# Two-block transformer layer pair on one core: where the token-form units of the second mixing accumulate

## What is computed

```python
u = rms_norm(h, ln_pre_mix[i])
proj = u @ w_in[i]
q_a, k_a, v_a, qkv_b, z_b, b_b, a_b, gate_a, gate_b = jnp.split(proj, IN_SPLITS, axis=-1)
qa = apply_rope(to_heads(q_a, 8), cos, sin)
ka = apply_rope(to_heads(k_a, 8), cos, sin)
y_a = from_heads(moba_attention(qa, ka, to_heads(v_a, 8)))        # plain causal attention at 256 tokens
qkv_b = jax.nn.silu(causal_depthwise_conv_2(qkv_b, conv_w[i]))    # 4 taps
q_b, k_b, v_b = jnp.split(qkv_b, 3, axis=-1)
o_b = gated_delta_rule(l2_norm(q_b), l2_norm(k_b), v_b, g_log, beta)
y_b = rms_norm(o_b, gdn_norm[i]) * jax.nn.silu(z_b)
merged = sigmoid(gate_a) * (y_a @ w_proj_a[i]) + sigmoid(gate_b) * (y_b @ w_proj_b[i])
```

## Time and profile before

| | us |
|---|---|
| median of the runs (3) | 1023.41 |
| the profiled execution | 1024.26 |
| its span, first to last instruction | 1022.0 |
| TensorE busy | 921.7 (90%) |
| VectorE busy | 584.3 (57%) |
| ScalarE busy | 523.7 (51%) |
| GpSimd busy | 133.2 (13%) |

### The profile page before, as it was taken

One profiled execution on the slowest core, in us unless ns is written; L12 is line 12 of the kernel. 1 busy time (PEld: TensorE's weight loads), 2 busy tenths in 40 slices (PEclk: granted clock), 3 DMA queues, 4 the chain that ended last, 5 costly groups with the idle time before them and its releaser, 6 DMA issues.

```text
span 1022.0 us, 16777 instructions
## 1 busy us (share of the span) xinstructions
PE 921.7 (90%) x6490; PEld 850.6 (83%) x6490; DVE 584.3 (57%) x865; ACT 523.7 (51%) x901; POOL 133.2 (13%) x122
## 2 busy tenths in 40 slices
PE   4996789999997988996898999998988999999977
PEld 4985589999996988996798988888976999999956
DVE  4576465555556556666546656463656555555555
ACT  5486454444447645554546363726336644444453
POOL 1000030000000000038536363300000000000000
PEclk9998989999998999999999999998999999999979
DMA  9631286656553444443212131312653555565611
GB/s 307 235 125 41 83 181 200 203 168 202 186 184 120 140 139 138 131 158 124 63 50 95 43 123 41 124 43 87 202 179 120 189 182 198 171 205 167 217 68 41
DMA packets 106940, 144.88 MB, mean 142 GB/s; under 512 B 2968, under 2 KB 94360, under 8 KB 106896
## 3 DMA queue, kind: packets, MB, share of 16 engines
q1 hardware_dynamic: 104608, 137.60, 42.0%
q0 software_dynamic: 1968, 6.02, 2.2%
q10 hardware_dynamic: 320, 0.66, 0.2%
HBM read 143.22 MB, written 1.05 MB: 141 GB/s over the span
## 4 chain that ended last, share of the span: by engine, by line
PE 75%; DVE 11%; ACT 9%; issue 3%; POOL 1%; DMA 1%; ACTq 0%; DVEq 0%; POOLq 0%
PE ps L1577 13%; PE ps L1579 13%; PE ps L1578 13%; PE ps L1583 8%; PE ps L1585 8%; PE ps L1584 8%; DVE wl L1090 3%; ACT wh L603 3%; PE ps L1897 2%; PE ps L1908 1%; PE ps L1912 1%; DVE R L1127 1%; PE ps L1729 1%; DVE h L1133 1%; DVE xTl L1117 1%
## 5 line engine op out<-in xcount | busy, mean ns | idle before, releaser
L1090 DVE TENSOR_TENSOR wl<-w_raw,wh 128x1024 fp32r<-128x1024 f32 x258 | 323.1, 1257 | 314.9 <-ACT wh L603 314.0
L1577 PE MATMUL ps<-xTh,wh 128*128 128x256 f32 (+1 forms) x1160 | 337.9, 291 | 13.3 <-ACT R L815 6.0
L1578 PE MATMUL ps<-xTl,wh 128*128 128x256 f32 (+1 forms) x1160 | 328.0, 283 | 0.0
L1579 PE MATMUL ps<-xTh,wl 128*128 128x256 f32 (+1 forms) x1160 | 327.8, 283 | 0.0
L603 ACT ACTIVATE wh<-w_raw 128x1024 fp32r<-128x1024 f32 x258 | 271.0, 1053 | 109.5 <-PE ps L1585 82.0
L1577 PEld LDWEIGHTS ps<-xTh,wh 128*128 128x128 f32 x1160 | 221.2, 191 | 18.9 <-ACT R L815 6.7
L1578 PEld LDWEIGHTS ps<-xTl,wh 128*128 128x128 f32 x1160 | 220.5, 190 | 2.1 <-issue 1.2
L1579 PEld LDWEIGHTS ps<-xTh,wl 128*128 128x128 f32 x1160 | 221.0, 191 | 0.0
L1583 PE MATMUL ps<-wh,y 128*128 128x512 f32 x224 | 89.4, 399 | 4.0 <-DVE y L1527 4.0
L1585 PE MATMUL ps<-wh,y 128*128 128x512 f32 x224 | 88.7, 396 | 0.0
L1584 PE MATMUL ps<-wl,y 128*128 128x512 f32 x224 | 88.3, 394 | 0.0
(11 more groups left out here) (337 smaller groups left out, 1331.7 us busy)
## 6 DMA issues: line engine op xcount, KB each, us to landing
w_raw<-in_w_in_dram SPq DMA_DIRECT2D x43, 1024.0 KB, 5.2
w_raw<-in_w_ff_dram SPq DMA_DIRECT2D x32, 1024.0 KB, 5.4
w_raw<-in_w_ffn_gate_dram SPq DMA_DIRECT2D x11, 1024.0 KB, 5.3
w_raw<-in_w_ffn_up_dram SPq DMA_DIRECT2D x11, 1024.0 KB, 5.3
w_raw<-in_w_ffn_down_dram SPq DMA_DIRECT2D x11, 1024.0 KB, 4.8
w_raw<-in_w_out_dram SPq DMA_DIRECT2D x8, 1024.0 KB, 4.9
w_raw<-in_w_proj_a_dram SPq DMA_DIRECT2D x4, 1024.0 KB, 4.9
w_raw<-in_w_proj_b_dram SPq DMA_DIRECT2D x4, 1024.0 KB, 5.0
```

Of the source, the lines that this page charges most:

```text
L1090: TT(split_view(wl, pu % UNITS, layout), raw_unit(SLOT[p], j, layout), split_view(wh, pu % UNITS, layout).bitcast(F32), ALU.subtract).then ...
L1577: mm(out, wh_, xh, start=first, stop=False)
L1578: mm(out, wh_, xl, start=False, stop=False)
L1579: return mm(out, wl_, xh, start=False, stop=last)
```

## The change

The token-form units no longer use the two unit banks. In the attention rounds (and in the set of units ahead of them) they accumulate in `acc[:, 0]` and `acc[:, 1]`, the banks of the scores; in the delta-rule rounds in `ma` and `mb`. So they neither wait for the unit banks nor fill them. A new semaphore `tok_out` counts ScalarE's copies of token-form results. TensorE waits for it where the borrowed banks are used next: the scores (stage 1 of an attention round), the sums of squares (stage 1 of a delta-rule round), `g_rows` and `out_transposes`. Before token-form units of a delta-rule round start, TensorE waits for `yb_lo` (or `o2_lo`) and `dt_out`, which say that `ma` and `mb` were read. The table of bank counts leaves the token form out. The number and size of all matmuls, copies and transfers is the same.

```diff
-            elif to in ("tok", "high") and j == 1:
+            elif to == "high" and j == 1:
...
+        tok_out = sem("token_rows_copied")
...
                 elif c == 7:
                     for t in range(NT):
-                        act.activation(va[:, t, :], fm[:, t, 0:S], ACT.Copy).then_inc(emptied[t], 1)
+                        ins = act.activation(va[:, t, :], acc[:, t, 0:S], ACT.Copy)
+                    ins.then_inc(tok_out, 1)
...
                     for t in range(NT):
-                        act.activation(zr[:, t, :], fm[:, t, 0:S], ACT.Copy).then_inc(emptied[t], 1)
+                        ins = act.activation(zr[:, t, :], acc[:, t, 0:S] if first else ps[:, 6 + t, 0:S], ACT.Copy)
+                    ins.then_inc(tok_out, 1)
...
                 if s == 15:
-                    act.wait_ge(emptied[0], along(EMPTIED0, 2 * P_GDN + 8, 8, a))
-                    act.wait_ge(emptied[1], along(EMPTIED1, 2 * P_GDN + 8, 8, a))
+                    act.wait_ge(tok_out, a + (PAIRS + 1))
...
-            def tok_steps(pu, off, stride=0, i=0):
+            def tok_steps(pu, off, banks, free, stride=0, i=0):
                 unit_ready(pu, stride, i)
                 j = pu % 2
                 if j == 0:
-                    bank_ready(0, pu, stride, i)
-                    bank_ready(1, pu, stride, i)
+                    free()
...
-                        last = three_tok(fm[:, t, 0:S], ...
+                        last = three_tok(banks[t], ...
...
+            def score_banks_free():
+                pass
+
+            def pair_steps(kinds, fu, stride, i, banks=(acc[:, 0, 0:S], acc[:, 1, 0:S]), free=score_banks_free):
...
             def moba_stage(s, a):
                 if s == 1:
                     pe.wait_ge(rope_out, a + 1)
+                    pe.wait_ge(tok_out, a + 1)
...
                         pe.wait_ge(sq_out, a * 2 + (n + 1))
+                        pe.wait_ge(tok_out, PAIRS + 1)
...
                 if s == 9 and not (isinstance(a, int) and a == PAIRS - 1):
+                    pe.wait_ge(tok_out, a + (PAIRS + 1))
                     g_rows(a + 1)
                 if s == 13 and not (isinstance(a, int) and a == 0):
+                    pe.wait_ge(tok_out, a + (PAIRS + 1))
                     out_transposes(a - 1)
...
+            def norm_banks_free(a):
+                def free():
+                    if isinstance(a, int) and a == 0:
+                        pe.wait_ge(o2_lo, PAIRS)
+                    else:
+                        pe.wait_ge(yb_lo, a)
+                    pe.wait_ge(dt_out, a + 2)
+                return free
+
             def pair_round(weave, stage, kinds, fu, a):
-                steps = pair_steps(kinds, fu, 8, a)
+                if weave is GDN_WEAVE:
+                    steps = pair_steps(kinds, fu, 8, a, (ma[:, 0:S], mb[:, 0:S]), norm_banks_free(a))
+                else:
+                    steps = pair_steps(kinds, fu, 8, a)
```

More of the change, by code:

```diff
@@ L825, in gdn_unit @@
                 unit_wait(fu, stride, a)
-                later = not (isinstance(pair, int) and pair == 0)
+                first = isinstance(pair, int) and pair == 0
+                later = not first
                 if c < 6:
@@ L1609, in tok_steps @@
                         k = 4 * j + kk
-                        last = three_tok(fm[:, t, 0:S], xTh[:, k, off + t * P:off + (t + 1) * P], xTl[:, k, off + t * P:off + (t + 1) * P],
+                        last = three_tok(banks[t], xTh[:, k, off + t * P:off + (t + 1) * P], xTl[:, k, off + t * P:off + (t + 1) * P],
                                          a[:, kk, :], b[:, kk, :], k == 0, k == KC - 1)
@@ L1802, in _ @@
             M, G = 2 * P_MOBA, 2 * P_GDN
-            def pair_steps(kinds, fu, stride, i):
+            def score_banks_free():
+                pass
+            def pair_steps(kinds, fu, stride, i, banks=(acc[:, 0, 0:S], acc[:, 1, 0:S]), free=score_banks_free):
                 for c in range(8):
                     if kinds[c] == "t":
-                        yield from tok_steps(fu + c, 0, stride, i)
+                        yield from tok_steps(fu + c, 0, banks, free, stride, i)
                     else:
```

## The result

The changed kernel takes 1027.69 us (median of 8 runs, 1024.83 to 1030.19), against 1024.03 us for the kernel before (8 runs, 1023.19 to 1025.34). The ratio is 1.0031, with a 95% interval of 1.0021 to 1.0041: 3.2 us slower (3.7 us by the two medians). The three runs of before that gave 1023.41 us are among its eight here. The forecast was 1024.9 us, in a range of 1019.0 to 1028.5. The profiled execution took 1024.83 us, with a span of 1023.0 us at a mean granted clock of 0.964; it is the shortest of the eight, so the profile shows the mechanisms but less than the median's loss. Its span is 1.0 us longer than before's, although the first wait of the second mixing, ahead of anything that was changed, ends 0.87 us sooner in it (319.64 instead of 320.51).

A forecast was written before the change was run, and what follows sets the result against it. TensorE was taken to bound the kernel only where nothing else is late, with other engines' chains setting round starts. -4.4 + 3.2 + 1.65 + 1.0 = +1.5 us on 1023.41 gave 1024.9 us, range 1019.0 to 1028.5.

The forecast's parts named there:

- What bounds each place: At round starts: chains on other engines bound rounds, so shorter TensorE stalls there gain nothing; L815 waits grow to 7.4 us.
- The gain of the token-form starts: Set ahead and attention rounds 0 to 3: token-form starts no longer wait for the unit banks, -4.4 us.
- nothing new waits there: Behind the token-form starts of the attention part: no new wait arises, so the 4.4 us gain stays whole.
- The hold: Three delta-rule rounds: VectorE's splits, 0.80 us sooner, block GpSimd's last convolution operation (2.04 instead of 1.09 us), +3.2 us.
- The rival of no hold: Delta-rule rounds: second split comes just behind GpSimd's last operation, which is not held; -2.2 us, 1021.2 us, chance 0.36.
- The clock: Longer TensorE stops halve the granted clock: one of two attention stops +1.65 us, two of three delta-rule stops +1.0 us.
- the one of the delta-rule rounds: Clock falls behind two of the three longer delta-rule stops, at 0.5 us each, +1.0 us.
- rival 2: GpSimd is held and the clock falls in each of five stops; +3.6 to +7.1 us, middle 1028.8 us, chance 0.20.
- a dearer clock: Part of the forecast's own chance, 0.07, in which clock falls cost more and the time lies above 1025.5 us.

The follow-up runs named there:

- The fills: Changed kernel with eight unused matmuls per stop: in attention rounds 0 to 2 alone, 0.9984 of before; in delta-rule rounds 1 to 3 alone, 0.9999.

## Why the prediction was right, and where it was off

**What bounds each place: right.** The waits at token-form starts are gone. The waits at round starts did not turn into time: the wait for ScalarE's first copy grew by 1.6 us (I had 1.4), as the chain through the rotary embedding starts at the end of the token units. In the delta-rule rounds the silu is released by GpSimd, before and after.

**The gain of the token-form starts: 0.8 us too high.** Of the -4.4 us the three attention rounds and the set ahead (3.6 us) are there: attention round 2 has 28.04 us from its third unit to the scores of round 3, where it had 28.98. The set ahead can't be compared in this profile, as its clock is lower there (0.91 against 0.95); at 0.95, in the profile with one split waiting, it has 40.42 us to the third unit of round 0, where before has 41.18. In attention round 3 the step "nothing new waits there" failed:

```profile
464.76 0.28 PE L1588 MATMUL ps<-wh,xTl 128*128 128x256 f32 x1
465.92 0.46 PE L1857 MATMUL ps<-R 128*128 128x128 f32 x2 [0.88 <-DVE R L1343]
```

```profile
465.23 0.54 DVE L1343 COPY R<-ps 128x384 f32<-128x384 f32 x1
```

Soon behind the token-form start (its first matmul is at 464.18) TensorE now waits for VectorE's copy of the transposed probabilities, which ends at 465.77. The copy stands behind two splits that took 4.09 us in all, with GpSimd's convolution running (two of 1.23 us would be 2.5 us). I had looked for what is late at the starts of the rounds and not behind the start of the token-form units; the copy was a row of the trace that I didn't read for this round. With one tap of convolution this wait is not there.

**The hold: right in mechanism, place and size.** Three times both operations are held, with lags of 0.07 to 0.14 us, as follows from moving the splits by 0.80 us. It costs 1.1 us a round (the chain from the sixth unit's copy takes 10.74 instead of 9.64 us), 3.3 us in all; the sum had 3.2. It was forecast as happening by 0.05 to 0.1 us of lag, which is little; that it did happen in all three rounds is in part luck. The Trainium skill (SBUF — State Buffer, Who interferes with whom) has the rule: one shared pair of ports, and issue order decides who is blocked. The trace agrees: an operation that starts 0.13 us behind a split takes 2.04 us and the split 1.22 us; before, where the split starts 0.83 us behind the operation, the operation takes 1.09 us and the split 1.34 us. The rival of no hold is out; it had 2.2 us less than before, and the kernel in which one split waits, the nearest to it, measured 1.8 us less.

**The clock: right in kind, probably too small.** The sum had +2.65 us (one fall at 1.65 and two at 0.5). The profile has one new fall in the two attention stops, as forecast, and one in the three delta-rule stops, where two were. With 3.6 and 3.3 us for the other two terms, the measured +3.2 us leaves 3.5 us for the clock in the timed runs; that is a remainder and not a measurement. The fills give 1.8 + 3.3 = 5.1 us, with 2 and 1.5 us of uncertainty. The term that looks mis-sized is the one of the delta-rule rounds, +1.0 us: filling their stops gave 3.3 us. How many falls the timed runs had there, and what each cost, is not shown. That about half of the stops would have a fall was a choice and no reading of a row: stops of equal length behaved differently.

So the changed kernel is slower by 3.2 and not by 1.5 us: 0.8 us from attention round 3, and by what is left about 0.9 us from the falls. For more than 2.05 us the forecast had a chance of 0.27: 0.20 in rival 2, the same mechanism with a fall in each of five stops, and 0.07 in a dearer clock. The median of 1027.69 us lies in that rival's range (from 1027.0 us, with its middle at 1028.8), but 0.6 us of it belong to the kernel before, whose median rose from 1023.41 to 1024.03 us with more runs. The change itself, +3.2 us, is below the rival's +3.6 and nearer to the forecast's +1.5 than to the rival's middle of +5.4 us. The rival's condition was not met in the profile, where two of the five stops had a fall. In the mean of the timed runs the clock was lower than there (0.9615 against 0.964), so they had more falls than the profile; how many of the five stops is not shown.

## What to carry to other kernels

A wait that ends sooner moves everything that follows it on other engines, too. Ask of each engine that follows the moved work (here VectorE's splits) what it shares with a chain that does not move (here GpSimd's convolution), and lay the two timelines over each other with the shift put in; all that kept 3.3 us away was that two splits started 0.75 and 0.83 us behind GpSimd's operations. Work that nobody waits for yet should stand behind a chain that someone does wait for: one wait of 3.4 us on VectorE in each of three rounds was worth 5 us, 2.8 of them by the hold itself. And stalls that can't be removed can be kept from costing twice by giving TensorE work in them.

## What was not expected of the hardware

Stops of equal length had different clocks behind them. The 2.3 us ahead of the third unit gave 0.87 in one round and 1.00 in the next of the same execution; 2.92 us gave 1.00, 0.89 and 1.00 in three rounds. Executions of one kernel differ by several us: 1024.83 to 1030.19 us for the changed kernel, with the longest at the lowest clock (0.954). Filling some stops does not by itself make this small (1019.49 to 1026.79 with the attention stops filled), and the narrowest, 1017.41 to 1018.76 us, is the kernel in which both splits wait and no stop is filled. Filling a stop of 3.0 us with 1.8 us of matmuls was enough in the profile (1.00 in the window behind it, with 1.2 us of idle time left). The kernel before had 3.0 us to win in its attention rounds by filling alone (1.0 us either way), nearly twice what its one visible fall costs in the profile (14.91 against 13.26 us); the profiled execution is only one of several.
